# The first tile after each layer norm computed on the unnormed residual, in a two-block transformer kernel

## The reference, cut to what matters

```python
def layer_norm(x, g, b):
    mu = jnp.mean(xf, axis=-1, keepdims=True)
    var = jnp.mean(jnp.square(xf - mu), axis=-1, keepdims=True)
    return ((xf - mu) * lax.rsqrt(var + LN_EPS) * g + b).astype(x.dtype)

for i in range(DEPTH_2):                       # 2 layers
    mix = nsa_pool_mixer(x, ...) if i % 2 == 0 else gla_mixer(x, ...)
    x = layer_norm(ALPHA * x + mix, ln1_g[i], ln1_b[i])
    x = layer_norm(ALPHA * x + sqrelu_mlp(x, mlp_w1[i], mlp_w2[i]), ln2_g[i], ln2_b[i])
```

## Time and profile before

| | |
|---|---|
| median of 3 runs | 1891.39 us (1889.86 to 1891.47) |
| profiled execution | 1891.13 us, span 1889.3 us |
| mean granted clock of TensorE | 0.998 of full speed |
| PE busy | 1866.1 us |
| DVE, ACT, POOL busy | 783.3, 433.6, 1078.6 us |
| DMA | 173.78 MB, mean 92 GB/s |

### The profile page before, as it was taken

One profiled execution on the slowest core, in us unless ns is written; L12 is line 12 of the kernel. 1 busy time (PEld: TensorE's weight loads), 2 busy tenths in 40 slices (PEclk: granted clock), 3 DMA queues, 4 the chain that ended last, 5 costly groups with the idle time before them and its releaser, 6 DMA issues.

```text
span 1889.3 us, 24381 instructions
## 1 busy us (share of the span) xinstructions
PE 1866.1 (99%) x8998; PEld 1511.8 (80%) x8998; DVE 783.3 (41%) x1278; ACT 433.6 (23%) x846; POOL 1078.6 (57%) x622
## 2 busy tenths in 40 slices
PE   7999999999999999999999999999999999999998
PEld 5878887888888888876778888887877878888887
DVE  6774433352342433687451212127833561212123
ACT  5223422310010122156140101023424140101020
POOL 5755762576757656520556655565862546666652
PEclk9999999999999999999999999999999999999999
DMA  6322321232333224210223332222331223332331
GB/s 228 110 79 90 107 94 45 90 100 90 114 99 112 92 83 146 81 56 1 67 84 96 99 100 89 89 90 89 102 98 46 73 95 101 102 102 95 100 101 45
DMA packets 47455, 173.78 MB, mean 92 GB/s; under 512 B 5264, under 2 KB 5904, under 8 KB 46736
## 3 DMA queue, kind: packets, MB, share of 16 engines
q1 hardware_dynamic: 46800, 169.54, 28.0%
q10 hardware_dynamic: 576, 3.11, 0.5%
HBM read 170.53 MB, written 2.10 MB: 91 GB/s over the span
## 4 chain that ended last, share of the span: by engine, by line
PE 97%; DVE 1%; ACT 1%; DMA 0%; issue 0%; SPq 0%; DVEq 0%
PE acc L516 17%; PE acc L517 17%; PE acc L518 17%; PE acc L543 6%; PE acc L540 6%; PE acc L539 6%; PE acc L595 1%; PE acc L998 1%; PE acc L597 1%; PE acc L596 1%; PE misc L1014 1%; PE misc L1034 1%; PE acc L1190 1%; PE acc L1192 1%; PE acc L1191 1%; PE acc L615 1%
## 5 line engine op out<-in xcount | busy, mean ns | idle before, releaser
L2642 POOL TENSOR_SCALAR w_hi<-raw 128x1024 fp32r<-128x1024 f32 x309 | 335.0, 1084 | 757.9 <-PE acc L543 277.6
L2644 POOL TENSOR_TENSOR w_lo<-raw,w_hi 128x1024 fp32r<-128x1024 f32 x309 | 748.3, 2422 | 25.8
L516 PE MATMUL acc<-x_hi,w_hi 128*128 128x512 f32 x872 | 340.1, 390 | 0.0
L518 PE MATMUL acc<-x_hi,w_lo 128*128 128x512 f32 x872 | 339.3, 389 | 0.0
L517 PE MATMUL acc<-x_lo,w_hi 128*128 128x512 f32 x872 | 339.3, 389 | 0.0
L1970 DVE TENSOR_TENSOR h<-acc,h 128x512 f32<-128x512 f32 x112 | 77.4, 691 | 357.3 <-PE acc L518 226.5
L516 PE MATMUL acc<-y_hi,w_hi 128*128 128x512 f32 x540 | 211.3, 391 | 0.0
L518 PE MATMUL acc<-y_hi,w_lo 128*128 128x512 f32 x540 | 210.1, 389 | 0.0
L517 PE MATMUL acc<-y_lo,w_hi 128*128 128x512 f32 x540 | 210.1, 389 | 0.0
L516 PEld LDWEIGHTS acc<-x_hi,w_hi 128*128 128x128 f32 x872 | 163.7, 188 | 34.2 <-issue 0.3
L518 PEld LDWEIGHTS acc<-x_hi,w_lo 128*128 128x128 f32 x872 | 163.7, 188 | 34.0
(11 more groups left out here) (479 smaller groups left out, 2800.5 us busy)
## 6 DMA issues: line engine op xcount, KB each, us to landing
raw<-weights_dram SPq DMA_DIRECT2D x309, 512.0 KB, 3.5
h<-x_dram SPq DMA_DIRECT2D x2, 1024.0 KB, 6.3
out_dram<-out_tok SPq DMA_DIRECT2D x6, 256.0 KB, 2.1
small<-small_dram SPq DMA_DIRECT2D x1, 1408.0 KB, 15.9
mem_in<-mem_dram SPq DMA_DIRECT2D x1, 1024.0 KB, 13.0
w_cmp<-w_cmp_dram ACTq DMA_DIRECT2D x1, 1024.0 KB, 6.9
small<-small_dram ACTq DMA_DIRECT2D x1, 992.0 KB, 4.8
const<-const_dram SPq DMA_DIRECT2D x1, 640.0 KB, 9.2
```

What stands on the lines that cost most here:

```text
L516: mm(out, m["w_hi"][:, slot, k], hi[:, k], start=k == 0, stop=False)
L518: last = mm(out, m["w_lo"][:, slot, k], hi[:, k], start=False, stop=k == kc - 1)
L2642: nc.gpsimd.tensor_scalar(hi, m["raw"][:, slot], 1.0, 0.0, ALU.mult, ALU.add).then_inc(sem("weights_high"), 1)
L2644: nc.gpsimd.tensor_tensor(m["w_lo"][:, slot].rearrange("p k n -> p (k n)"), m["raw"][:, slot], bf(hi), ALU.subtract).then_inc(sem("weights ...
```

## The change

The first tile of the stage behind each of the three norms is no longer part of the opening. It runs on `h * g` where `h` is the unnormed, partly centred residual: for `y = ((h - mu) * r * g + b) W` is `r * ((h * g) W) - r * mu * (g W) + b W`. So:

- ScalarE writes `x_hi[k]` = high part of `h * g` behind each square, VectorE `x_lo[k]` in `plain_low(k)`: four of them after the squares of chunk 4 are added, those of chunks 4, 5 and 6 each in its step of the residual loop, the last one after the first scaled chunk.
- TensorE adds 16 products of four columns (`plain_columns`) between L652 and L654: the tile's weights by `-g/D` and by `b`, in high and low parts. The four filler products go. The tile's 24 products come next, then the opening of tiles 1, 2, 3; `dense` starts with tile 4.
- ScalarE copies the four column sums and the mean out of PSUM; `x_hi[k]` is overwritten by the normed chunk when the plain tile has read it. VectorE, before the third scaled chunk (whose bank is now that of the plain tile), applies the mean and the factor (`plain_fix`) into `z`; ScalarE puts it back into the bank, with the bias, after all chunks are kept.
- The MLPs' first group leaves TensorE's loop and is written out.

```diff
-        fourth = (START[BEFORE_STAGE[name]] + 3) % RING
+        fourth = (START[BEFORE_STAGE[name]] + (0 if name in LAYER_NORMS else 3)) % RING
...
+    def plain_opening(norm):
+        i, first = LAYER_NORMS.index(norm), START[BEFORE_STAGE[norm]]
+        slot = first % RING
+        claim(first)
+        for k in range(KC):
+            pe.wait_ge(sem("plain_ready"), KC * i + k + 1)
+            mm(acc[:, slot], m["w_hi"][:, slot, k], x_hi[:, k], start=k == 0, stop=False)
+            mm(acc[:, slot], m["w_hi"][:, slot, k], x_lo[:, k], start=False, stop=False)
+            last = mm(acc[:, slot], m["w_lo"][:, slot, k], x_hi[:, k], start=False, stop=k == KC - 1)
+            last.then_inc(sem("plain_read" if k < KC - 1 else "tile_done"), 1)
+        pe.wait_ge(sem("plain_cols_out"), i + 1)
+        opening(first + 1, first + 1, norm)
+
+    def plain_columns(norm):
+        i, first = LAYER_NORMS.index(norm), START[BEFORE_STAGE[norm]]
+        slot = first % RING
+        out = acc[:, (first + 1) % RING, 0:4]
...
+        for k in range(KC):
+            mm(out, m["w_hi"][:, slot, k], m["gb_r"][:, k], start=k == 0, stop=False)
+            last = mm(out, m["w_lo"][:, slot, k], m["gb_r"][:, k], start=False, stop=k == KC - 1)
+        last.then_inc(sem("plain_cols"), 1)
...
+        plain_columns(name)
         pe.wait_ge(sem("tile_out"), first)
         mm(misc[:, 0, :], ones, m["h"][:, KC - 1], start=False, stop=True).then_inc(sem("ln_mean"), 1)
         pe.wait_ge(sem("norm_sq"), chunks_before(name) + KC)
         mm(summed, ones, m["sq"][:, (KC - 1) % 2], start=False, stop=True).then_inc(sem("norm_summed"), 1)
-        idle_products(4, first % RING)
...
+        def plain_high(k):
+            f(m["x_hi"][:, k], m["h"][:, k], ACT.Copy, scale=pr.col(gain, at + k)).then_inc(sem("plain_high"), 1)
...
+        act.wait_ge(sem("plain_cols"), i + 1)
+        f(m["gb_cols"], acc[:, (first + 1) % RING, 0:4], ACT.Copy).then_inc(sem("plain_cols_out"), 1)
...
+        f(m["mean"], misc[:, 0, :], ACT.Copy).then_inc(sem("plain_mean"), 1)
...
+        act.wait_ge(sem("plain_fixed"), i + 1)
+        act.wait_ge(sem("norm_kept"), KC * (KEPT.index(name) + 1))
+        own.link(f(acc[:, first % RING], z[:, first % RING], ACT.Identity, bias=m["gb_sum"][:, 1:2]))
...
+        def plain_low(k):
+            dve.wait_ge(sem("plain_high"), KC * i + k + 1)
+            v.scalar_tensor_tensor(m["x_lo"][:, k], h[:, k], pr.col(gain, at + k), bf(m["x_hi"][:, k]),
+                                   ALU.mult, ALU.subtract).then_inc(sem("plain_ready"), 1)
+
+        def plain_fix():
+            slot = first % RING
+            dve.wait_ge(sem("plain_cols_out"), i + 1)
+            own.mark(v.tensor_tensor(m["gb_sum"], m["gb_cols"][:, 0:2], m["gb_cols"][:, 2:4], ALU.add))
+            dve.wait_ge(sem("tile_done"), first + 1)
+            own.settle()
+            own.link(v.scalar_tensor_tensor(z[:, slot], m["mean"], m["gb_sum"][:, 0:1], acc[:, slot], ALU.mult, ALU.add))
+            v.tensor_tensor(z[:, slot], z[:, slot], rstd, ALU.mult).then_inc(sem("plain_fixed"), 1)
...
             if k < KC - 1:
                 add_squares(name, k)
+            if k == HALF:
+                for early in range(HALF):
+                    plain_low(early)
             if k == KC - 2:
                 for x, (whole, parts) in enumerate(((part, "sum_hl"), (rstd, "sq_hl"))):
                     dve.wait_ge(sem("ln_high"), 2 * i + x + 1)
                     v.tensor_tensor(m[parts][:, 1], whole, bf(m[parts][:, 0]), ALU.subtract).then_inc(sem("ln_low"), 1)
+            if k < KC - 1:
+                plain_low(k)
...
+        dve.wait_ge(sem("plain_mean"), i + 1)
         centred = [centre(k) for k in range(2)]
...
         def scale(k):
+            if k == 2:
+                plain_fix()
             own.settle(centred[k])
...
         def next_centre(k):
             if k + 2 < KC:
                 centred.append(centre(k + 2))
+            if k == 0:
+                plain_low(KC - 1)
```

More of the change, by code:

```diff
@@ L340, in memory_map @@
     place("ones_r", [P], F32R, region(4 * P))
+    place("gb_r", [KC, 4], F32R, region(4 * 4 * KC))
+    place("gb_f", [KC], F32, region(4 * KC))
+    place("gb_cols", [4], F32, region(16))
+    place("gb_sum", [2], F32, region(8))
     small = region(4 * max(columns(SMALL1)[1], columns(SMALL2)[1]))
@@ L522, in dense @@
                 after(k)
+    def plain_opening(norm):
[14 more added lines that the diff above has]
+        out = acc[:, (first + 1) % RING, 0:4]
+        pe.wait_ge(sem("weights_split"), first + 1)
+        pe.wait_ge(sem("tile_out"), first - 2)
+        pe.wait_ge(sem("plain_gb"), i + 1)
+        for k in range(KC):
+            mm(out, m["w_hi"][:, slot, k], m["gb_r"][:, k], start=k == 0, stop=False)
+            last = mm(out, m["w_lo"][:, slot, k], m["gb_r"][:, k], start=False, stop=k == KC - 1)
+        last.then_inc(sem("plain_cols"), 1)
     def opening(t0, first_tile, norm):
@@ L627, in stage @@
             late_opening(START[name], START[name], norm)
-        elif norm:
-            opening(START[name], START[name], norm)
-        for i in range(3 if norm else 0, n):
+        elif norm in LAYER_NORMS:
+            plain_opening(norm)
+        for i in range(4 if norm in LAYER_NORMS else 3 if norm else 0, n):
             t = START[name] + at + i
@@ L1102, in mlp_group @@
         t0 = g * 16 + START[name]
-        opening(t0, START[name], norm)
-        for j in range(3, 8):
+        plain = isinstance(g, int) and g == 0
+        if plain:
+            plain_opening(norm)
+        else:
+            opening(t0, START[name], norm)
+        for j in range(4 if plain else 3, 8):
             dense(t0 + j, (START[name] + j) % RING, x_hi, x_lo)
@@ L1114, in mlp @@
     def mlp(name, norm, high, next_norm=None):
-        with pe.Fori(0, GROUPS - 1) as g:
+        mlp_group(name, 0, norm, high)
+        with pe.Fori(1, GROUPS - 1) as g:
             mlp_group(name, g, norm, high)
@@ L1385, in residual_ln @@
         i = LAYER_NORMS.index(name)
+        gain, at = name[:3] + "_g", KC * (name[3] == "b")
+        first = START[BEFORE_STAGE[name]]
+        def plain_high(k):
+            f(m["x_hi"][:, k], m["h"][:, k], ACT.Copy, scale=pr.col(gain, at + k)).then_inc(sem("plain_high"), 1)
         for k in range(HALF):
@@ L1388, in residual_ln @@
             square(name, k, m["h"])
+            plain_high(k)
         rstd, _, banks = pr.norm_banks(name)
@@ L1397, in residual_ln @@
             square(name, k, m["h"])
+            plain_high(k)
+        act.wait_ge(sem("plain_cols"), i + 1)
+        f(m["gb_cols"], acc[:, (first + 1) % RING, 0:4], ACT.Copy).then_inc(sem("plain_cols_out"), 1)
         act.wait_ge(sem("ln_mean"), 2 * i + 2)
         f(m["sq"][:, 0], misc[:, 0, :], ACT.Square, scale=1.0 / D).then_inc(sem("ln_mean_sq"), 1)
+        f(m["mean"], misc[:, 0, :], ACT.Copy).then_inc(sem("plain_mean"), 1)
         act.wait_ge(sem("ln_var"), i + 1)
         rsqrt(rstd, rstd, 1.0, LN_EPS, "norm_rstd")
-        bias, at = name[:3] + "_b", KC * (name[3] == "b")
+        bias = name[:3] + "_b"
         alpha_b = m["alpha_b"][:, 16 * (name[2] == "2"):]
         def high(k):
+            if k < KC - 1:
+                act.wait_ge(sem("plain_read"), (KC - 1) * i + k + 1)
+            else:
+                act.wait_ge(sem("tile_done"), first + 1)
             f(m["x_hi"][:, k], banks[k % 3], ACT.Identity, bias=pr.col(bias, at + k)).then_inc(sem("norm_high"), 1)
@@ L1905, in residual_ln @@
         rstd, summed, banks = pr.norm_banks(name)
+        gain, at = name[:3] + "_g", KC * (name[3] == "b")
+        first = START[BEFORE_STAGE[name]]
+        gb, bias = m["gb_r"], pr.view(name[:3] + "_b")[:, at:at + KC]
+        own.mark(v.tensor_scalar(m["gb_f"], pr.view(gain)[:, at:at + KC], -1.0 / D, None, ALU.mult))
+        own.mark(v.tensor_copy(gb[:, :, 1], bias))
+        own.settle()
+        own.mark(v.tensor_copy(gb[:, :, 0], m["gb_f"]))
+        own.mark(v.tensor_tensor(gb[:, :, 3], bias, bf(gb[:, :, 1]), ALU.subtract))
+        own.settle()
+        v.tensor_tensor(gb[:, :, 2], m["gb_f"], bf(gb[:, :, 0]), ALU.subtract).then_inc(sem("plain_gb"), 1)
+        def plain_low(k):
[7 more added lines that the diff above has]
+            dve.wait_ge(sem("tile_done"), first + 1)
+            own.settle()
+            own.link(v.scalar_tensor_tensor(z[:, slot], m["mean"], m["gb_sum"][:, 0:1], acc[:, slot], ALU.mult, ALU.add))
+            v.tensor_tensor(z[:, slot], z[:, slot], rstd, ALU.mult).then_inc(sem("plain_fixed"), 1)
         for k in range(HALF):
@@ L1937, in residual_ln @@
                     v.tensor_tensor(m[parts][:, 1], whole, bf(m[parts][:, 0]), ALU.subtract).then_inc(sem("ln_low"), 1)
+            if k < KC - 1:
+                plain_low(k)
         dve.sem_inc(sem("norm_added"), 1)
-        gain, at = name[:3] + "_g", KC * (name[3] == "b")
         dve.wait_ge(sem("norm_summed"), NORMS.index(name) + 1)
```

## The result

The changed kernel takes 1927.64 us (median of 4 runs, 1926.08 to 1930.32), the kernel before on the same chip 1891.43: ratio 1.020, 95% interval 1.0188 to 1.0213. It is 36.2 us slower. The forecast was 28.6 us slower, 1920, range 1897 to 1932.

The account below looks back on a forecast made before the run. TensorE was taken to bound the kernel, holding 97% of the last chain. Per norm 8.8 - 1.9 + 2.5 = 9.4 us; three norms and 0.4 for gla_in make 28.6 us slower, 1920 us, range 1897 to 1932.

Parts of the forecast that it names:

- plain_low and ScalarE's waits, clean: Seven added VectorE operations and waits for ScalarE, less 0.89 us slack, put each norm's last residual add 4.3 us later.
- port waits: plain_low, with two SBUF inputs, and GpSimd's weight splits block each other before the last add: 3.5 us per norm.
- columns: 16 four-column products on TensorE ahead of the last two sums, partly hidden by the last add: 1.0 us later per norm.
- C: The moment in each norm when TensorE starts the last two sums; forecast to come 8.8 us later.
- after C: From the last two sums' start to the fifth tile's start: 25.9 us instead of 27.83, a gain of 1.9 per norm.
- clock: TensorE's standstill of 3.5 to 7.5 us before the low parts' sums most likely halves its clock: 2.5 us per norm.
- the stall: TensorE waits 1.6 us in the opening's second chunk for its low part, delayed by plain_fix on VectorE.
- the bank's wait: TensorE waits under 1 us before the fifth tile, which needs the first tile's bank, free at C + 25.9.
- (d): Rival: port waits in full (4.4) and clock lost for two stretches: 12 us per norm, 1927 to 1932; chance 0.15.
- (b): Rival: no port waits and the clock holds: 2.7 us per norm, 1899 us; chance 0.15.
- (c): Rival: port waits but full clock: 6.9 us per norm, 1912 us; chance 0.2.
- (a): Rival: the tile fills the gap as meant, the last add stays at 945.57: 1885 to 1891 us; chance 0.1.

Follow-up runs that it names:

- e1: The changed kernel with the first seven plain_low of each norm subtracting a PSUM bank instead of x_hi (one SBUF input); ratio 1.011 to the kernel before.
- e3b: The changed kernel with 7 filler products on TensorE in front of the wait for the low parts; ratio 1.0251 to the kernel before.
- e8: The change in the two norms ahead of the MLPs only, the norm ahead of gla_in as before; ratio 1.0134 to the kernel before.

## Why the prediction was right, and where its sizes were off

The first norm's 11.57 us, split by the runs; e1 gives the port, e3b the same instructions at full clock:

```
                                              forecast  measured  from
plain_low and ScalarE's waits, clean            4.3       3.4     low sums at +3.61 (e1) instead of +0.23
port waits                                      3.5       4.2     +7.84 instead of +3.61
columns                                         1.0       2.0     low sums to C 3.04 (e3b) instead of 1.02
after C                                        -1.9      -1.9     25.97 (e3b) instead of 27.83
clock                                           2.5       3.8     5.11 - 3.04, and 27.70 - 25.97
sum                                             9.4      11.6
```

At full clock the 16 products take 1.7 us (0.11 each), and the low sums 0.3 longer than before. In the other two norms the clock's share, by e3b, is 3.1.

The mechanism was right, and every step that I named is in the trace of the first norm. The sizes were off: 28.6 us forecast, 37.3 measured, 3.2 of the difference in gla_in, for a reason that I had not seen.

- **VectorE ahead of the last add** was the step that decided, and it went as described: a stretch without idle time, and the add 8.4 us later where I had 7.8. Without port waits it is 4.1 later (e1: 4.63 us after the last residual product instead of 0.50), against my 4.3. The table has 3.4 because the low sums wait for six of the seven `plain_low` only; I had let all seven count. This and the port waits are two thirds of the size (7.6 of 11.6) and give the sign.
- **Port waits.** I had 1.1 and 4.4 as bounds and took 3.5; it was 4.2. The walk through the two splits was right almost to the row: the five end at 945.9 (I had 945.8), the sixth waits 1.3 us. The Trainium skill, "SBUF — State Buffer", section "Who interferes with whom", has two SBUF inputs on VectorE as the condition; e1 bears it out, since one input fewer ended it.
- **Columns.** The term was half of what it should be, 1.0 for 2.0: I had let the last add hide 0.9 of them, but it ended at 954.83, with the low sums, and the columns began at 954.96, so that nothing was hidden. The bounds, 0.7 to 1.9, held for the products.
- **After C** at full clock 25.97 us against the 25.9 that I worked out. In the first norm the stall was 1.41 (I had 1.6) and the bank's wait 0.51 (I had 0.7); in the changed kernel's other two norms the stall was only 0.37 and 0.54, and the bank's wait in ln1b 1.35, over the 1 us that I had named.
- **Clock.** The largest miss of a term, 3.8 for 2.5. I had named the case (low sums, columns, last sums and the start of the plain tile all inside, up to 4) and didn't take it. The standstill was 7.45 us, the upper end of what I had; the clock fell 5 us before its end and came back 8.6 us behind it.
- **gla_in, not foreseen**: 0.4 forecast, for the gate's product, which waited for nothing; 3.6 measured, further in. VectorE's gate chain there runs on SBUF inputs beside GpSimd's splits. From the first gate operation to the last k_g it took 44.1 us before (1333.47 to 1377.58) and 47.6 after (1355.98 to 1403.61); the scan of the first head, 1.94 before, now takes 3.30 (the first two rows are from the kernel before):

```profile
1336.39 1.94 DVE L2493 TENSOR_TENSOR_SCAN gb<-small,gz 128x512 f32<-128x512 f32 x1
...
1377.58 2.11 DVE L2511 TENSOR_TENSOR k_g<-k_g,z 128x512 f32<-128x512 f32 x1 [0.70 <-ACT z L1730]
...
1357.58 3.30 DVE L2581 TENSOR_TENSOR_SCAN gb<-small,gz 128x512 f32<-128x512 f32 x1
...
1403.61 1.02 DVE L2599 TENSOR_TENSOR k_g<-k_g,z 128x512 f32<-128x512 f32 x1 [0.70 <-ACT z L1784]
```

So the scores, which had no wait before, wait 1.84 us, and the clock falls behind that:

```profile
1404.69 0.69 PE L1241 MATMUL misc<-q_g,kt_g 128*64 128x64 f32 x16 [1.84 <-DVE k_g L2599]
```

```profile
1402.50:1405.00 2.50, 0.66 (x12) 0.31 (x12) 1.44 (x2) 2.05 (x5) 1.87 (x2) 1.00 0.61 210
1405.00:1409.00 4.00, 4.00 (x26) 3.31 (x21) 0.84 (x2) 1.13 (x3) 1.85 (x1) 0.57 0.25 76
```

e8 shows that it comes of ln2a's change. The rows show how: in both kernels GpSimd does eight splits in a row behind the opening. Before, they begin 8.7 us ahead of the first gate operation (1324.79), since the fourth tile runs beside the first of them, and end 24.6 us into the chain; now they begin 3.6 us ahead of it (1352.38) and end 30.0 us into it. That these 5 us of overlap make the 3.5 us is argued only: no run moved the splits alone.

The outcome, 1927.6, lies where rival (d) had it, 12 us per norm and 1927 to 1932, and not in the forecast's own 1916 to 1926: the port waits near their full size and the clock in full. That it meets (d)'s number is in part luck: the norms alone cost 11.2 us each, which gives 1925, and the rest is gla_in, which no rival had. (b) and (c) fall with the rows above, (a) with the add at 954.14. Port and columns 1.7 short, the clock 1.3, gla_in 1.1 (3.2 over three norms), less 0.9 for the clean part, are 3.2 us per norm; ln2a, 1.1 us cheaper than the first, brings the mean to the 2.9 that 37.3 less 28.6 makes.

## What to carry to other kernels

Ahead of the instruction that ends a dependency chain a busy engine has no free slot, however low its share over the span: read the timeline of that stretch, and put new work behind the instruction or on another engine (26.6 of the 36.2 us were the place of seven instructions). A product moved into a gap gains only by what the gap has after everything that came along with it; here 2.4 of 5.44 us, and only once nothing else waited. A wait of TensorE can cost more than itself: here 3.1 to 3.8 us on top of 7.45, and in four of ten executions 1.7 on top of 1.84, since the clock falls behind it.

## What the hardware showed that I had not expected

- Where VectorE's operations with two SBUF inputs meet GpSimd's splits, VectorE loses most: 2.95 us over five, GpSimd 0.41 + 0.30.
- A product of 4 columns with a full weight load costs 0.11 us at full clock, 0.213 at half, and 0.12 at full clock when put between products that use the same weights: nothing is saved by standing next to them.
- The wait of 1.84 us in gla_in occurs in all ten kernels of the table in which ln2a is changed, but the granted clock behind it fell in four of the profiled executions only (0.66 to 0.71 over 5 us). The rest of gla_in shows it as two values, 194.7 and 196.3 us. With two like stretches elsewhere (at about 127 and 837 us, there in some executions and not in others) such falls, 1.7 us each, are probably a part of the spread between runs; the profiled executions alone can't show how large a part.
